# One core, a two-layer decoder trunk: the block compression as 16 products a set, both latent norms as one chain, the query up-projections emptied by two engines

## The reference, cut to what matters

```
h = rmsnorm(x); z = h @ w_in            # 18 column groups for four parallel mixers
# mixer 1, sparse attention (2 key/value heads of 64): blocks of 32 tokens, every 16 tokens, so 31 blocks
blocks = x[:, cidx] + pe;  kc = einsum('bclhd,lde->bche', blocks, w)   # once for keys, once for values
# then attention in three passes: over the 31 compressed blocks, over selected tokens, over a window
# mixer 2, sliding window;  mixer 4, forgetting attention
# mixer 3, latent attention: c_q has 256 channels, c_kv 128
q  = rmsnorm(c_q)  @ w_q_up    # 8 heads x (64 plain + 32 rotary)
kv = rmsnorm(c_kv) @ w_kv_up   # 8 heads x (64 key + 64 value)
# each mixer's output -> @ w_branch_i, times sigmoid(h @ w_gate_i), summed, @ w_out, norm, added to x
# then cross-attention into 256 memory rows, then the SwiGLU feed-forward, both with norms around them
```

## Time and profile before

| what | value |
|---|---|
| median of 3 runs | 2753.11 us (2752.0 to 2753.18) |
| the profiled execution's own time | 2754.73 us |
| its span, first to last instruction | 2753.1 us |
| PE busy | 2479.9 us (90%), 13342 matmul records |
| PE weight loads busy | 2037.3 us (74%) |
| DVE busy | 1597.9 us (58%) |
| ACT busy | 1163.0 us (42%) |
| POOL busy | 187.8 us (7%) |
| mean granted TensorE clock | 0.945 of 2.4 GHz |

### The profile page before, as it was taken

One profiled execution on the slowest core, in us unless ns is written; L12 is line 12 of the kernel. 1 busy time (PEld: TensorE's weight loads), 2 busy tenths in 40 slices (PEclk: granted clock), 3 DMA queues, 4 the chain that ended last, 5 costly groups with the idle time before them and its releaser, 6 DMA issues.

```text
span 2753.1 us, 42467 instructions
## 1 busy us (share of the span) xinstructions
PE 2479.9 (90%) x13342; PEld 2037.3 (74%) x13342; DVE 1597.9 (58%) x3572; ACT 1163.0 (42%) x2432; POOL 187.8 (7%) x225
## 2 busy tenths in 40 slices
PE   2899899999999879999968988998999997899997
PEld 1686777778787657888857677787888775688886
DVE  3457887676375665553244688676736756555422
ACT  1325656464354452222222466455625545322222
POOL 3300000000000230000030000000000022100000
PEclk8879999999999989999978999999999998899998
DMA  4511112222313203333342111222131241133332
GB/s 80 130 39 40 32 47 62 62 62 66 82 53 115 77 24 91 96 94 95 96 94 73 39 40 32 62 62 62 49 97 54 77 130 32 54 94 97 97 92 71
DMA packets 343965, 196.34 MB, mean 71 GB/s; under 512 B 29340, under 2 KB 338704, under 8 KB 343152
## 3 DMA queue, kind: packets, MB, share of 16 engines
q1 hardware_dynamic: 340512, 178.02, 22.7%
q0 software_dynamic: 3280, 16.13, 2.6%
HBM read 186.78 MB, written 7.34 MB: 71 GB/s over the span
## 4 chain that ended last, share of the span: by engine, by line
PE 78%; DVE 10%; issue 5%; ACT 3%; DMA 2%; POOL 1%; DVEq 0%; ACTq 0%; POOLq 0%; SPq 0%
PE acc L1060 60%; PE o_acc L1060 5%; PE turn L1204 3%; PE scores L1060 2%; PE acc L1344 2%; PE scores L1189 1%; DMA w_f<-in_w_in_dram 1%; DVE trunk L1535 1%; DVE ring L1621 1%; PE scores L1190 1%; DVE w_lo L1465 1%; ACT w_hi L743 1%; DMA head_sink<-in_swa_sinks_dram 1%; DVE p_lo L1561 1%; PE scores L1125 1%
## 5 line engine op out<-in xcount | busy, mean ns | idle before, releaser
L1060 PE MATMUL acc<-h_hi,w_hi 128*128 128x512 f32 x1888 | 772.3, 409 | 94.2 <-DVE h_lo L1522 64.8
L1060 PE MATMUL acc<-h_lo,w_hi 128*128 128x512 f32 x1888 | 757.2, 401 | 0.0
L1060 PE MATMUL acc<-h_hi,w_lo 128*128 128x512 f32 x1888 | 755.2, 400 | 0.0
L1465 DVE TENSOR_TENSOR w_lo<-w_f,w_hi 128x1024 fp32r<-128x1024 f32 x336 | 414.2, 1233 | 538.6 <-ACT w_hi L743 537.5
L1060 PEld LDWEIGHTS acc<-h_hi,w_hi 128*128 128x128 f32 x1888 | 366.9, 194 | 177.8 <-issue 62.9
L743 ACT ACTIVATE w_hi<-w_f 128x1024 fp32r<-128x1024 f32 x336 | 353.1, 1052 | 307.9 <-PE acc L1060 266.0
L1060 PEld LDWEIGHTS acc<-h_hi,w_lo 128*128 128x128 f32 x1888 | 366.5, 194 | 78.4
L1060 PEld LDWEIGHTS acc<-h_lo,w_hi 128*128 128x128 f32 x1888 | 367.2, 194 | 65.8
L858 ACT ACTIVATE ring<-ring,neg_max 128x256 f32<-128x256 f32 (+4 forms) x416 | 209.6, 504 | 175.6 <-DVE neg_max L1621 174.3
L1204 PE MATMUL turn<-ident,ring 128*128 128x128 f32 (+1 forms) x880 | 167.9, 277 | 34.3 <-DVE ring L1644 18.0
L795 ACT ACTIVATE p_hi<-turn 128x256 fp32r<-128x256 f32 (+4 forms) x326 | 128.3, 393 | 153.5 <-PE turn L1204 150.2
(11 more groups left out here) (270 smaller groups left out, 3853.4 us busy)
## 6 DMA issues: line engine op xcount, KB each, us to landing
w_f<-in_ffn_w_in_dram SPq DMA_DIRECT2D x88, 512.0 KB, 3.8
w_f<-in_w_gate_dram SPq DMA_DIRECT2D x64, 512.0 KB, 4.1
w_f<-in_w_in_dram SPq DMA_DIRECT2D x62, 512.0 KB, 3.9
w_f<-in_w_branch_dram SPq DMA_DIRECT2D x32, 512.0 KB, 3.4
w_f<-in_ffn_w_out_dram SPq DMA_DIRECT2D x32, 512.0 KB, 4.1
w_f<-in_w_out_dram SPq DMA_DIRECT2D x16, 512.0 KB, 4.3
w_f<-in_ffn_w_out_dram SPq DMA_DIRECT2D x16, 384.0 KB, 3.5
x_spill<-trunk POOLq DMA_DIRECT2D x2, 2048.0 KB, 8.4
```

The source lines that it names most:

```text
L1060: ins = nc.tensor.matmul(dst, a, b, start=(n == 0 and not added), stop=(n == count - 1))
L1465: nc.vector.tensor_tensor(w_lo[:, u % 2, :], w_f32[:, u % 2, :], w_hi[:, u % 2, :].bitcast(F32), ALU.subtract).then_inc(w_ready, 1)
```

## The change

Five edits go together:

1. **Compression.** Two positions of a block lie on the 128 partitions (position parity times 64 channels), so a set is 16 float32 matmuls of 128x64 weights on 64 columns (two heads times 31 blocks and the position term). `block_w` for both sets lies in `wide`; POOL writes no zeros and issues two DMAs a layer in place of four. The gather is twelve half-width copies a set: DVE makes the keys' set, before `rotate_key`, and ACT the values' set, after its last `nsa` unit. DVE empties the compressed sets within the loop over `h` chunks, after chunks 3 and 4, and the values are transposed by two matmuls.
2. **Start of CMP.** PE no longer waits for all eight chunks of `h` but for each at its first use, and `Pass.ahead` for CMP is 36 (it was 24); its rate stays 3.
3. **Latent norms.** One norm "mla" with eight columns (four for queries, four for keys/values): ACT makes the three squares in a row, after the split of `br1` unit 1; PE does all sums at once, before `br1` unit 1, and all rows in one go after its first 12 matmuls, into two banks; POOL takes one power of eight columns.
4. **`qup`.** ACT and DVE both wait for PE's chunk and empty their halves side by side; PE waits for both. The next unit's split comes after the first chunk of a unit, not before it.
5. **`kvup`.** PE additionally waits for DVE's last two `qup` chunks; nothing else changes.

```diff
-        self.ahead = 24 if name == "cmp" else 12
+        self.ahead = 36 if name == "cmp" else 12
...
-        return -(-(24 * (n + 1) - self.ahead) // self.rate) - 1
+        return max(-(-(24 * (n + 1) - self.ahead) // self.rate) - 1, -1)
...
-        block_w = [wide_flat.rearrange("p (l e) -> p l e", l=CMP_LEN), block_wv]
-        block_in = [proj[:, c:c + 2, :].rearrange("p a b -> p (a b)").rearrange("p (l c) -> p l c", l=CMP_LEN)
+        pairs = CMP_LEN // 2
+        block_w = [wide_flat[:, cv * pairs * HD:(cv + 1) * pairs * HD].rearrange("p (m e) -> p m e", m=pairs)
+                   for cv in range(2)]
+        block_in = [proj[:, c:c + 2, :].rearrange("p a b -> p (a b)").rearrange("p (m k c) -> p m k c", m=pairs, k=KVH)
...
+        def block_copies(l, cv, copy):
+
+            src = proj[:, PJ_K["cmp"] + cv, :]
+            pe_cols = cmp_pe[:, bass.ds(l * (2 * CMP_LEN) + cv * CMP_LEN, CMP_LEN)].rearrange("p (m t) -> p t m", t=2)
+            for t in range(2):
+                to = slice(t * HD, (t + 1) * HD)
+                for kv in range(KVH):
+                    for half in range(2):
+                        at = half * CMP_STRIDE
+                        copy(block_in[cv][to, half * 8:(half + 1) * 8, kv, 0:NC],
+                             src[kv * HD:(kv + 1) * HD, at:at + NC * CMP_STRIDE].rearrange(
+                                 "p (c m t) -> p t m c", m=8, t=2)[:, t, :, :]).then_inc(blocks_tok[cv], 1)
+                for kv in range(KVH):
+                    copy(block_in[cv][to, :, kv, NC], pe_cols[to, t, :]).then_inc(blocks_tok[cv], 1)
 
...
-                    for kv in range(KVH):
-                        a, b = kv * HD, (kv + 1) * HD
-                        c, d = (1 - kv) * HD, (2 - kv) * HD
-                        pool.memset(block_w[cv][a:b, :, c:d], 0.0).then_inc(blocks_zero, 1)
-                        pool.dma_start(block_w[cv][a:b, :, a:b],
-                                       nsa_cmp_w[l, cv].rearrange("n d e -> d n e")).then_inc(blocks_in[cv], 16)
-                wait_apart(pool, blocks_zero, l * 4 + 4)
-                power(l, "mlaq")
-                power(l, "mlakv")
+                    pool.dma_start(block_w[cv], nsa_cmp_w[l, cv].rearrange("(m t) d e -> (t d) m e", t=2)
+                                   ).then_inc(blocks_in[cv], 16)
+                power(l, "mla")
...
-                    for c in range(2):
-                        square_chunk(l, "mlaq", c, latent(c))
-                    for k in range(2):
-                        next_unit(l, "br1", k, 0)
+                    next_unit(l, "br1", 0, 0)
+                    act.wait_ge(summed, l * NSQ + SQB["mla"] + 2)
+                    act.wait_ge(rbc_ready, l * NNORM + (NB_OF["mla"] + 1))
+                    for c, dst in enumerate((squares[:, 0, :], squares[:, 1, :], square_sum[:, :])):
+                        nc.scalar.activation(dst, latent(c), ACT.Square).then_inc(squared, 1)
+                    next_unit(l, "br1", 1, 0)
                     for c in range(2):
                         split_chunk(l, "mlaq", c, v_hi[:, c, :], latent(c))
-                    square_chunk(l, "mlakv", 0, latent(2))
                     next_unit(l, "br1", 2, 0)
                     split_chunk(l, "mlakv", 0, v_hi[:, 2, :], latent(2))
                     act.wait_ge(turned_raw[0], l * 80 + 80)
...
+                wait_chunk_read(act, l, "nsa", PJ_V["cmp"])
+                block_copies(l, 1, lambda dst, src: nc.scalar.activation(dst, src, ACT.Copy))
...
-                    if k == 0:
-                        act.wait_ge(turned_raw[1], l * 80 + 80)
-                    next_unit(l, "qup", k, 0)
                     for n in range(4):
                         c = 4 * k + n
-                        act.wait_ge(rope, l * 12 + (6 + c))
+                        if n == 1:
+                            if k == 0:
+                                act.wait_ge(turned_raw[1], l * 80 + 80)
+                            next_unit(l, "qup", k, 0)
+                        wait_chunk(act, l, "qup", k, 0, n)
                         nc.scalar.activation(proj[0:HD, c, :], acc[(CB["qup"] + c) % 2][0:HD, :], ACT.Copy,
                                              scale=-(HD + ROT) ** -0.5).then_inc(acc_free[(CB["qup"] + c) % 2], 1)
...
+            def latent_sums(l):
+
+                at = l * NSQ + SQB["mla"]
+                pe.wait_ge(squared, at + 3)
+                token_columns(PART_SUMS, squares[:, 0, :], part_sums)
+                for i in range(NT):
+                    nc.tensor.matmul(SUMS[:, i:i + 1], squares[:, 1, i * P:(i + 1) * P], ones[:, 0:1],
+                                     start=True, stop=True)
+                token_columns(SUMS[:, NT:2 * NT], square_sum, token_sums)
+
+            def latent_rows(l):
+
+                pe.wait_ge(rstd_split, l * NNORM + NB_OF["mla"] + 1)
+                for g, bank in enumerate((RBC, RBC_KV)):
+                    for i in range(NT):
+                        col = g * NT + i
+                        for m, part in enumerate((rstd_hi, rstd_lo)):
+                            ins = nc.tensor.matmul(bank[:, i * P:(i + 1) * P],
+                                                   part[:, col:col + 1].to_broadcast([P, P]), ident_r[:, :],
+                                                   start=(m == 0), stop=(m == 1))
+                ins.then_inc(rbc_ready, 1)
+
...
+                            first = ps is CMP and n == 0
+                            unit_terms(l, name, k, 0, a, b, when_split(l, "mix_norm", h_rhs) if first else h_rhs)
...
-                early_sums(l, "mlaq")
-                last_sums(l, "mlaq")
+                latent_sums(l)
                 unit_terms(l, "br1", 1, 0, 0, 12, y_rhs)
-                spread_rows(l, "mlaq")
+                latent_rows(l)
                 unit_terms(l, "br1", 1, 0, 12, 24, y_rhs)
-                last_sums(l, "mlakv")
-                unit_terms(l, "br1", 2, 0, 0, 12, y_rhs)
-                spread_rows(l, "mlakv")
-                unit_terms(l, "br1", 2, 0, 12, 24, y_rhs)
+                whole_unit(l, "br1", 2, 0, y_rhs)
                 whole_unit(l, "br1", 3, 0, y_rhs)
-
...
-                    pe.wait_ge(blocks_in[cv], l * 32 + 32)
-                    if cv == 0:
-                        pe.wait_ge(blocks_zero, l * 4 + 4)
-                    pe.wait_ge(blocks_tok, l * 6 + 3 * (cv + 1))
+                    pe.wait_ge(blocks_in[cv], l * 16 + 16)
+                    pe.wait_ge(blocks_tok[cv], l * 12 + 12)
                     pe.wait_ge(acc_free[c % 2], free_at(l, c, 1, 0))
-                    for n in range(CMP_LEN):
-                        ins = nc.tensor.matmul(acc[c % 2][:, 0:NCP], block_w[cv][:, n, :], block_in[cv][:, n, :],
-                                               start=(n == 0), stop=(n == CMP_LEN - 1))
+                    for n in range(pairs):
+                        ins = nc.tensor.matmul(acc[c % 2][0:HD, 0:KVH * NCP].rearrange("p (k c) -> p k c", k=KVH),
+                                               block_w[cv][:, n, :], block_in[cv][:, n, :, :],
+                                               start=(n == 0), stop=(n == pairs - 1))
                     ins.then_inc(part_ready, 1)
...
                 wait_chunk_read(pe, l, "cmp", 1)
                 wait_apart(pe, ng_tanh, l + 1)
-                wait_split(l, "mix_norm", KT)
...
-                project(l, "qup", lambda kt: (v_hi[:, kt, :], v_lo[:, kt, :]))
+                for c in range(8):
+                    if c >= 2:
+                        pe.wait_ge(rope, l * 12 + (4 + c))
+                    unit_terms(l, "qup", c // 4, 0, 6 * (c % 4), 6 * (c % 4) + 6,
+                               lambda kt: (v_hi[:, kt, :], v_lo[:, kt, :]))
                 wait_split(l, "mlakv", 1)
-                project(l, "kvup", lambda kt: (v_hi[:, 2, :], v_lo[:, 2, :]))
+                for c in range(8):
+                    if c < 2:
+                        pe.wait_ge(rope, l * 12 + (12 + c))
+                    unit_terms(l, "kvup", c // 4, 0, 3 * (c % 4), 3 * (c % 4) + 3,
+                               lambda kt: (v_hi[:, 2, :], v_lo[:, 2, :]))
                 wait_chunk_read(pe, l, "kvup", 7)
...
+            def latent_means(l):
+
+                dve.wait_ge(part_sums, l * len(PART_OF) + PART_OF["mla"] + 1)
+                nc.vector.tensor_scalar(mean_part[:, :], PART_SUMS[:, 0:NT], 1.0 / QR, EPS, ALU.mult,
+                                        ALU.add).then_inc(mean_parted, 1)
+                dve.wait_ge(token_sums, l * NNORM + NB_OF["mla"] + 1)
+                nc.vector.tensor_scalar(mean_sq[:, NT:2 * NT], SUMS[:, NT:2 * NT], 1.0 / KVR, EPS, ALU.mult, ALU.add)
+                dve.wait_ge(mean_parted, l * len(PART_OF) + PART_OF["mla"] + 1)
+                nc.vector.scalar_tensor_tensor(mean_sq[:, 0:NT], SUMS[:, 0:NT], 1.0 / QR, mean_part[:, :], ALU.mult,
+                                               ALU.add).then_inc(ms_ready, 1)
```

(38 more changed lines are left out.)

99 lines of the change are left out of this document (42 added, 57 removed).

## The result

The changed kernel took 2736.56 us (four runs, 2734.05 to 2738.12) beside 2752.6 for the kernel before on the same chip. The ratio is 0.9941, 95% interval 0.9924 to 0.9958. So it is faster, by 16 us. Forecast were 35 us, 2718 with a range of 2708 to 2731: the prediction missed. Its profiled execution has a span of 2735.1 us.

What follows compares the result with a forecast made beforehand. PE was taken as the bound, carrying 78% of the chain that ended last. Savings of 12.0 + 0.8 + 1.7 + 3.0 = 17.5 us a layer, 35 for two, took 2753.1 to 2718 us, range 2708 to 2731.

Steps and rivals of the forecast that it cites:

- the clock does not come back in CMP's steps: Rival: low clock through the first 36 matmuls and 32 CMP steps behind the new idle time; 2828 us, chance 3%.
- part 1: Compression and start of CMP: first score 12.0 us a layer earlier, and net 0.8 us from CMP's steps.
- the 0.9 us that PE waits: CMP step 4: unit 2 of the gates not yet split by DVE when PE's filler wants it; stall of 0.9 us.
- CMP's steps: Last four steps without filler give back 1.7 us, less a 0.9 stall: net 0.8 us a layer.
- the new idle time ahead of the filler: PE idle from 163.8 to about 171.3 us, between compression and filler, waiting for tanh; expected to lower the clock.
- its price of 55 us a layer: Cost of the 3% low-clock rival: 4.9 + 50 us a layer, a CMP step of 1.55 us becoming 3.1.
- Part 1, front: First compression matmul to CMP's first score: 12.0 us a layer saved, with 36 filler matmuls ahead of the score.
- the limit I had set was 14.5: Sign of being wrong: tanh coming later than 14.5 us after the first compression matmul.
- POOL's lost memsets and two lost DMAs I cost at nothing: Early nsa projections: fewer POOL writes and loads worth 0, since PE waited for DVE's gather and not for them.
- Part 2: Latent norms in branch 1: both PE waits go, 1.7 us a layer saved; POOL's eight-column power taken as 1.6 us.
- Part 3: Up-projections: qup saves 2.1 us and kvup's first stalls shrink by 0.9, together 3.0 us a layer.
- The two stalls behind the splits: In qup, the bank DVE empties after a split comes 0.85 us late for PE, twice.

Runs made afterwards that it cites:

- e9: The changed kernel run again, unchanged; six executions: 2708.0, 2709.1, 2710.7, and 2734.8, 2735.0, 2739.4 us.
- e7: Changed kernel, 36 filler matmuls ahead, with unit 2 of the gates split by ACT and DVE before CMP's first step; 2709.1 us, ratio 0.9837.
- e3: Kernel before with only the filler ahead of CMP's first score raised from 24 to 36 matmuls; 2809.4 us, ratio 1.0204.
- e13: Changed kernel, stall left in, plus 26 unread matmuls in the idle time before the filler; four executions 2731.2 to 2735.2 us, eight 2760.9 to 2762.6.
- e5: Kernel before with only the latent norms made one chain; 2752.9 us, ratio 0.9997.
- e6: Kernel before with only the up-projections changed, emptied by ACT and DVE side by side; 2746.2 us, ratio 0.9971.
- e4: Kernel before with only the compression change and PE's separate waits for chunks of h, 24 filler matmuls ahead; 2719.1 us, ratio 0.9874.
- e11: As e7, with three br1 matmuls after each of the first two eights of norm sums, rows after 18 terms; 2707.1 us, ratio 0.9829.
- e12: As e7, with 26 unread 512-column matmuls between the compression and tanh; 2702.0 us, ratio 0.9809.
- e1: Changed kernel with 24 filler matmuls ahead of CMP's first score, not 36; its last reading: place in time alone, either may happen; 2710.4 us, ratio 0.9842.
- e14: e11 and e12 together: early split, spread sums and filled idle time, 36 ahead; 2702.5 us, ratio 0.9814.

## Why the prediction was wrong

**The step that failed** is the rival that I put at 3%, "the clock does not come back in CMP's steps". Against it I had set that "the same steps were at full clock in the old kernel". They were, but without a stall of PE among them. I had found the stall myself, in part 1, and priced it as the 0.9 us that PE waits. In the sum it stands as the 0.9 taken off CMP's steps, net 0.8. Its size was right: PE idled 0.90 us, and e9's CMP is 1.1 and 1.0 us longer than e7's in the two layers. What I left out is that a wait inside CMP's steps puts the clock itself at stake, and that the steps, once low, stay low to their end: 27.5 us for a wait of 0.9. The rival was wrong in two things. I had tied it to the new idle time ahead of the filler; e3 and e13 show that this idle time isn't needed. And its price of 55 us a layer took a step of 1.55 us as 3.1 at the low clock; measured was 2.73 (median from one step's score to the next), and 27.5 for the layer. The Trainium skill, page "TensorE: Matmul & The Clock Gate", section "HAM oscillation — how this bites in real kernels", tells of waits of PE that bring the low clock; its case is waits for DMA at each tile, and no run here has one of that kind in CMP.

The other steps, by the two profiles:
- **Part 1, front.** Forecast 12.0 a layer with 12 more matmuls in it, measured 12.5 and 11.5. Inside it terms were off and cancelled. A record costs 0.107 us at the low clock and 0.058 at the full one (forecast 0.11), and the clock rose during the sets, so both took 5.5 us and not 7. DVE's copies took 3.0 in place of 2.6, the empties 0.4 each and not 0.5. Tanh started 13.1 us after the first product; the limit I had set was 14.5. The low clock took 3.9 and 5.8 us of the filler (4.6).
- **Part 1, "POOL's lost memsets and two lost DMAs I cost at nothing".** This is wrong too, in the kernel's favour. In the `nsa` projections of the kernel before PE waits for DVE's split of a weight unit, which waits for its load, and that load stands beside POOL's block loads. These are the waits of layers 0 and 1 in the kernel before:
```profile
PE acc L1060 <- DVE w_lo L1465: 3.8, 1, 3.8
...
PE acc L1060 <- DVE w_lo L1465: 2.6, 1, 2.6
```
In the changed kernel the same two waits are:
```profile
PE acc L1077 <- DVE w_lo L1510: 1.8, 1, 1.8
...
PE acc L1077 <- DVE w_lo L1510: 1.0, 1, 1.0
```
In e5 and e6, which load as before, they stay at 2.7 and 3.6 to 3.8. By the positions of PE's matmuls in e4, whose two waits are also 1.8 and 1.0, the stretch gives 2.1 and 3.2 us, 5.3 in all. The waits are 3.6 of it; the rest goes with the low clock behind them, which stood there for 6.8 and 3.4 us in the kernel before and for 3.4 and 0 in e4. That the fewer loads do it is the likely reading; no run isolates them.
- **CMP's steps.** Net 0.8 forecast, 1.1 measured in layer 1 (46.0 to 44.9), apart from the clock.
- **Part 2.** 1.7 forecast; 0.45 and 1.24 in the two layers of the changed kernel. Both waits did go, as forecast, but the low clock behind the sums took 0.8 where it came, and POOL's power of 2.5 us, for which I had taken 1.6, is what e11's chain shows in front of the rest.
- **Part 3.** 3.0 forecast, 2.5 measured. The two stalls behind the splits are there as priced (0.85 forecast, 0.8 each); the row of the changed kernel that answers to the earlier trace rows is PE's now, since ACT no longer waits for DVE:
```profile
PE acc L1077 <- DVE proj L1835: 1.6, 2, 0.8
```
Of the missing 0.5, 0.3 lies in `kvup`, which gave 0.6 and not 0.9, and 0.2 in `qup`, which gave 1.9 and not 2.1.

Without the fall the parts give 16.6 and 16.3 us in the two layers, near the forecast 17.5, and with the 5.3 of the loads 38. The undisturbed executions of the changed kernel were 44 us faster than before (2709 to 2753.6); the 6 us left fit the short stretches of low clock that came or went elsewhere, as in e6 and e12. Had the clock stayed in every execution, the forecast of 2718 would have been too high by 9, within its range.

**What stays open.** Why the same program with the same stall keeps the clock in one execution and loses it in another, and why e13 and e3 lose it more often than the changed kernel. The traces give a lead, and no more. Eight profiled passes have PE idle for 0.9 us at this place. Counted from the last rise of the clock to the start of that idle time, the fallen ones stand at 11.3 us (changed kernel, layer 0), 11.3 and 11.0 (e3), 11.1 and 24.2 (e13); the kept ones at 10.2 (changed kernel, layer 1), 11.5 and 10.2 (e9). So the stall is needed, but tenths of a microsecond of its place in time may decide, as e1's last reading had it. No run moves the stall by such steps.

## What to carry to other kernels

Where PE is the bound and its clock is high, look for the first wait that a change adds among short, mixed steps: its price is not its length but, with some chance, the low clock for all the work up to the next dense stretch (here 27.5 us for 71.7 us of it). When work is moved ahead of a pass, everything due by its count (here a weight unit's split) comes due earlier too; move the split with it. And when a loss comes in one of two equal layers, run the same program again before looking for a difference between the layers.

## What the runs showed of the hardware

- The clock fell 1.5 us after PE resumed from a 0.9 us wait (182.25 to 183.76; 1.5 to 2.2 in the other four such passes, of e3 and e13) and then stayed at 0.50 for 71.7 us with PE busy for 71.25 of 71.60. Before, it had risen 3.9 us after the filler's matmuls of 512 columns began at 166.2.
- At the low clock a step of CMP took 2.73 us in place of 1.55, and the pass 72.4 in place of 44.9: less than twice as long.
- One program has two times, about 2709 and 2736: none of the 10 executions of the changed kernel lies between 2711 and 2734.
- Records of one column, 24 in a row with PE never idle, had 3.4 us of low clock behind them in 13 of 20 profiled passes (both of e5, neither of e12); with three matmuls of 512 columns after each of the first two eights, in none of four (e11, e14).
- A float32 record with 64 weight columns and 64 moving ones took 0.107 us at 1.2 GHz and 0.058 at 2.4 GHz; with 128 weight columns and 32 moving ones it had taken 0.215 at 1.2 GHz.
- ACT and DVE, reading different partitions of one PSUM bank at the same time, took 0.59 and 0.69 us for 512 columns, as long as one behind the other.
- POOL's power took 1.04 us for four columns and 2.5 for eight: more than twice.
